# Spreading a gathered token's row into four PSUM banks at once, and sharing three banks between the U and V sums

## The reference

```
q = (t @ wq)                            # 8 heads, 2 halves of 128
s = q . keys ; top 16 of each half ; top 16 of the sums     -> eid, fv
g = softmax(fv)                          # 8 heads x 16 experts per token
hid = gelu(sum_d t[d] * u_tab[eid, d])   # d = 2048
out = sum_e (g * hid)[e] * v_tab[eid, :]
```

## Time and profile before

| what | value |
|---|---|
| median of three executions | 2251.37 us |
| the profiled execution's own time | 2247.8 us |
| its span, first to last instruction | 2246.0 us |
| TensorE busy in the span | 2175.7 us (97%) |
| VectorE busy | 1668.7 us (74%) |
| ScalarE busy | 916.3 us (41%) |
| GpSimd busy | 399.9 us (18%) |
| mean granted clock of TensorE | 0.994 of full speed |

### The profile page before, as it was taken

The page is one execution under the profiler, slowest core; times in us unless marked ns, Lnnn a source line. Parts: engine busy times, 40 slices in busy tenths (PEclk is TensorE's granted clock), DMA queues, the critical chain, the costliest instruction groups (busy, mean ns, idle before and its releaser), DMA issues.

```text
span 2246.0 us, 37321 instructions
## 1 busy us (share of the span) xinstructions
PE 2175.7 (97%) x14886; PEld 1927.0 (86%) x14886; DVE 1668.7 (74%) x3054; ACT 916.3 (41%) x1093; POOL 399.9 (18%) x337
## 2 busy tenths in 40 slices
PE   7899999899999999999999999999999999999996
PEld 1599888678799899999998888999888888989996
DVE  3269777654557899888878878787887877876686
ACT  1332323453443148444434434444343443444444
POOL 1044001300000046011122222222122221211000
PEclk9899999999999999999999999999999999999998
DMA  9957665798844465788899899999999999988763
GB/s 400 416 218 298 261 270 213 297 353 309 356 155 151 153 216 224 275 287 301 310 347 364 339 380 345 352 358 342 358 366 346 361 356 357 338 313 300 284 207 117
DMA packets 113334, 673.49 MB, mean 300 GB/s; under 512 B 12337, under 2 KB 13745, under 8 KB 50321
## 3 DMA queue, kind: packets, MB, share of 16 engines
q1 hardware_dynamic: 77184, 444.63, 52.6%
q0 software_dynamic: 33648, 219.49, 25.8%
q10 hardware_dynamic: 2336, 7.05, 0.8%
HBM read 649.17 MB, written 21.95 MB: 299 GB/s over the span
## 4 chain that ended last, share of the span: by engine, by line
PE 84%; DVE 7%; DMA 6%; ACT 1%; issue 1%; SPq 0%; POOL 0%; DVEq 0%; ACTq 0%
PE vb L1724 17%; PE zb L1709 15%; PE vb L1726 7%; PE zb L1711 7%; PE zb L550 6%; PE zb L552 5%; PE zb L551 5%; PE vb L1758 3%; PE vb L1748 3%; DMA ada_first<-in_w_ada 3%; PE vb L1308 2%; PE vb L1689 2%; PE zb L1665 1%; DVE lo L490 1%; PE vb L1555 1%; PE vb L1723 1%
## 5 line engine op out<-in xcount | busy, mean ns | idle before, releaser
L485 ACT ACTIVATE hi<-raw_two 128x1024 fp32r<-128x1024 f32 x624 | 657.1, 1058 | 966.3 <-PE vb L1724 308.4
L490 DVE TENSOR_TENSOR lo<-raw_two,hi 128x1024 fp32r<-128x1024 f32 x624 | 764.3, 1230 | 276.8 <-ACT hi L485 272.4
L1709 PE MATMUL zb<-act_hl,hi 128*128 128x416 f32 x1792 | 556.4, 368 | 0.0
L1724 PE MATMUL vb<-w_rest,hi 128*128 128x416 f32 x1536 | 495.3, 367 | 0.0
L1711 PE MATMUL zb<-act_hl,lo 128*128 128x208 f32 x1680 | 435.5, 259 | 0.0
L1709 PEld LDWEIGHTS zb<-act_hl,hi 128*128 128x128 f32 x1792 | 334.9, 188 | 35.9 <-issue 24.3
L1726 PE MATMUL vb<-w_rest,lo 128*128 128x208 f32 x1280 | 329.8, 258 | 0.0
L1711 PEld LDWEIGHTS zb<-act_hl,lo 128*128 128x128 f32 x1680 | 320.4, 191 | 5.2
L1724 PEld LDWEIGHTS vb<-w_rest,hi 128*128 128x128 f32 x1536 | 288.5, 188 | 1.4
L550 PE MATMUL zb<-act_hl,hi 128*128 128x288 f32 x960 | 287.8, 300 | 0.4 <-DVEq L1999 0.4
L551 PE MATMUL zb<-act_hl,hi 128*128 128x288 f32 x960 | 282.5, 294 | 0.0
(11 more groups left out here) (301 smaller groups left out, 2721.5 us busy)
## 6 DMA issues: line engine op xcount, KB each, us to landing
raw_two<-in_v SPq DMA_DIRECT2D x128, 1024.0 KB, 7.1
raw_two<-in_u SPq DMA_DIRECT2D x112, 1024.0 KB, 6.4
raw_two<-in_w_in SPq DMA_DIRECT2D x40, 1024.0 KB, 9.6
ada_first<-in_w_ada SPq DMA_DIRECT2D x64, 512.0 KB, 8.7
ada_mid<-in_w_ada SPq DMA_DIRECT2D x64, 512.0 KB, 5.3
ada_late<-in_w_ada SPq DMA_DIRECT2D x64, 512.0 KB, 7.3
raw_two<-in_w_out SPq DMA_DIRECT2D x16, 1024.0 KB, 6.1
raw_two<-in_w_q SPq DMA_DIRECT2D x16, 1024.0 KB, 4.9
```

The source lines that it names most:

```text
L485: act.activation(hi[s][:, :], raw[4 * (q % 2) + s], ACT.Copy).then_inc(hi_ready, 1)
L490: dve.tensor_tensor(lo[4 * (q % 2) + s][:, :], raw[4 * (q % 2) + s], hi[s][:, :].bitcast(F32), ALU.subtract) \
L1709: last = pe.matmul(zb[:, bank, 0:2 * ND], w_h, act_hl[:, k, :, 0:ND], start=(k == 0), stop=(k == KC - 1))
L1724: last = pe.matmul(vb[:, bank, 0:2 * ND], v_h, w[:, e % 2, :, :], start=(e == 0), stop=(e == GI - 1))
```

## The change

The four pieces of a token are spread at once into the four banks of `zb`, and VectorE takes them in one dot of 2048. The U and V sums move out of `zb` and share banks 3, 0 and 1 of `vb` in turn (`SUM_BANKS`), each waiting for the bank's user three places before (`wait_bank`). `add_halves` treats one bank at a time, so there are two for a U quad. All 80 tokens' rows now have the form that the last 16 had: five `twice` tiles, five calls of `turn_tokens`, and `pick_tail` in place of `pick`. The parts of `hid_4` and their reduction are gone. The first two U quads stay in `zb`; the last group's V sums go to `zb`, and the final norm's sum to `vb`.

```diff
-def chunk_unit(c):
-    return 53 * c // 48 - 8
+def spread_unit(t):
+    return 53 * (4 * t + 3) // 48 - 8
...
+SUM_BANKS = (3, 0, 1)
+def z_slot(p, e):
+    if p < PP:
+        return 2 * (p - 2) + e
+    return 4 + 24 * (p // PP - 1) + (e if p % PP == 0 else 16 + 2 * (p % PP) + e)
+def v_slot(g, c):
+    return 4 + 24 * (g - 2) + 2 + c
+def z_bank(p, e):
+    return zb[:, 2 * p + e, :] if p < 2 else vb[:, SUM_BANKS[z_slot(p, e) % 3], :]
+def v_bank(g, c):
+    return vb[:, c % 2, :] if g < 2 else vb[:, SUM_BANKS[v_slot(g, c) % 3], :]
...
 # GpSimd, after the spill of x
-            pool.wait_ge(hs_turned, 1)
-            pool.tensor_copy(twice[:, :, :, :], hF[:, :, ND + NR:T].unsqueeze(2).to_broadcast([P, KC, 2, NT])) \
-                .then_inc(twice_ready, 1)
+            for i in range(5):
+                if i == 4:
+                    pool.wait_ge(hs_turned, 1)
+                tokens = hF[:, :, ND + NT * i:ND + NT * i + NT]
+                pool.tensor_copy(twice[i][:, :, :, :], tokens.unsqueeze(2).to_broadcast([P, KC, 2, NT])) \
+                    .then_inc(twice_ready, 1)
...
 # GpSimd, in the dense loop
-                    for c in chunks_at(n):
-                        t = c // 4
-                        if c % 4 == 3 and t + 2 < NGT:
-                            pool.wait_ge(dots_done, c + 1)
+                    for t in spreads_at(n):
+                        if t + 2 < NGT:
+                            pool.wait_ge(dots_done, t + 1)
                             gather(ug[t % 2], u_rows, t + 2, ug_in[t % 2])
...
 # ScalarE
-                    for r in (0, NR):
-                        last = act.activation(pick[r:r + NR, :], ident[r:r + NR, r:r + NR], ACT.Copy)
-                    last.then_inc(hs_copied, 1)
...
 # TensorE
-            for k in range(KC):
-                for r in (0, NR):
-                    last = pe.matmul(vb[r:r + NR, k // 4, P * (k % 4):P * (k % 4) + P], hF[:, k, ND:ND + NR], ident,
-                                     start=True, stop=True)
+            def turn_tokens(i, bank):
+                pe.wait_ge(twice_ready, i + 1)
+                for kk in range(4):
+                    for j in range(4):
+                        both = twice[i][:, 4 * j + kk, :, :].rearrange("p s t -> p (s t)")
+                        last = pe.matmul(vb[2 * NT * j:2 * NT * j + 2 * NT, bank, P * kk:P * kk + P], both, ident,
+                                         start=True, stop=True)
+                return last
+            for i in range(4):
+                last = turn_tokens(i, i)
             last.then_inc(hs_turned, 1)
-            def turn_tail():
-                pe.wait_ge(twice_ready, 1)
-                for k in range(KC):
-                    j, kk = k // 4, k % 4
-                    last = pe.matmul(vb[2 * NT * j:2 * NT * j + 2 * NT, 2, P * kk:P * kk + P],
-                                     twice[:, k, :, :].rearrange("p s t -> p (s t)"), ident, start=True, stop=True)
-                last.then_inc(hs_turned, 1)
...
-            turn_tail()
+            turn_tokens(4, 2).then_inc(hs_turned, 1)
...
+            def wait_bank(m):
+                if m in (1, 2):
+                    pe.wait_ge(vb_free, 2 + 2 * KC - 2 + m)
+                elif m >= 3:
+                    i, r = divmod(m - 3 - 4, 24)
+                    if m - 3 < 4:
+                        pe.wait_ge(z_sum, 4 + m - 3 + 1)
+                    elif 2 <= r < 2 + KC:
+                        pe.wait_ge(vb_free, 2 + KC * (i + 2) + r - 2 + 1)
+                    else:
+                        pe.wait_ge(z_sum, 8 + 8 * i + (r if r < 2 else r - KC) + 1)
...
-            def spread_row(c):
-                if c == 0:
-                    pe.wait_ge(hs_copied, 3)
+            def spread_token(t):
+                if t == 0:
+                    pe.wait_ge(hs_split, 3)
+                    pe.wait_ge(z_sum, 4)
                 else:
-                    pe.wait_ge(dots_done, c)
...
-                pe.matmul(vb[:, 3, :], one.to_broadcast([P, P]), rows, start=True, stop=True).then_inc(spread, 1)
+                    pe.wait_ge(dots_done, t)
+                i, tt = t // NT, t % NT
+                rows = h_rows[i // 2][:, i % 2, :] if i < 4 else h_tail[:, :]
+                for j in range(4):
+                    last = pe.matmul(zb[:, j, :], pick_tail[:, j, tt:tt + 1].to_broadcast([P, P]), rows, start=True, stop=True)
+                last.then_inc(spread, 1)
...
 # VectorE
-                        rest = h_rows[b2][NR:ROWS, :, :]
-                        dve.tensor_tensor(rest, vb[NR:ROWS, 2 * b2:2 * b2 + 2, :], rest.bitcast(F32), ALU.subtract) \
+                        rows = h_rows[b2][:, :, :]
+                        dve.scalar_tensor_tensor(rows, vb[:, 2 * b2:2 * b2 + 2, :], lo_rows[:, 0:1], rows.bitcast(F32),
+                                                 ALU.mult, ALU.subtract).then_inc(hs_split, 1)
...
-                dve.wait_ge(unit_used, 4 * q + 8)
-                halves = zb[:, 2 * b:2 * b + 2, 0:2 * ND].rearrange("p e (h t) -> p e t h", h=2)
-                dve.tensor_reduce(zs[b][:, :, :], halves, AX_X, ALU.add).then_inc(z_sum, 1)
+                dve.wait_ge(unit_used, 4 * q + 2 * e + 6)
+                halves = z_bank(p, e)[:, 0:2 * ND].rearrange("p (h t) -> p t h", h=2)
+                dve.tensor_reduce(zs[p % 2][:, e, :], halves, AX_X, ALU.add).then_inc(z_sum, 1)
...
-            def dot(c):
-                t, j = c // 4, c % 4
+            def dot(t):
                 b = t % 2
-                dve.wait_ge(spread, c + 1)
-                u = ug[b][:, 512 * j:512 * j + 512]
-                dve.tensor_tensor_reduce(u, u, vb[:, 3, :], 1.0, 0.0, ALU.mult, ALU.add, hid_4[:, c % 64:c % 64 + 1]) \
-                    .then_inc(dots_done, 1)
+                dve.wait_ge(ug_in[b], 8 * (t - b) + 16)
+                dve.wait_ge(spread, t + 1)
+                dve.tensor_tensor_reduce(ug[b][:, :], ug[b][:, :], zb[:, :, :].rearrange("p j x -> p (j x)"), 1.0, 0.0,
+                                         ALU.mult, ALU.add, hid_s[:, t:t + 1]).then_inc(dots_done, 1)
...
-                    if s == 3:
-                        add_halves(q, PP * (g - 2) + pp, pp)
+                    if s >= 2:
+                        add_halves(q, PP * (g - 2) + pp, s - 2)
```

More of the change, by code:

```diff
@@ L112, with spreads_at @@
 LAST_QUADS = 32 * (NG - 3) - 12
-def chunks_at(n):
-    return [c for c in range(4 * NGT) if chunk_unit(c) == n]
+def spreads_at(n):
+    return [t for t in range(NGT) if spread_unit(t) == n]
 def tokens_at(n):
@@ L272, in layer_kernel @@
     vg = [at(f"vg{b}", [P, D], F32, peer + 76160 + 8192 * b) for b in range(2)]
-    h_rows = [at(f"h_rows{b}", [ROWS, 2, 512], F32R, (x_at + 14336, peer + 67968)[b]) for b in range(2)]
+    h_rows = [at(f"h_rows{b}", [P, 2, 512], F32R, (x_at + 14336, peer + 67968)[b]) for b in range(2)]
     h_tail = at("h_tail", [P, 512], F32R, peer + 72064)
-    twice = at("twice", [P, KC, 2, NT], F32, peer + 74112)
-    pick = at("pick", [ROWS, NR], F32R, peer + 96768)
+    twice = [at(f"twice{i}", [P, KC, 2, NT], F32, zone + 45568 + 2048 * i if i < 4 else peer + 74112) for i in range(5)]
     pick_tail = at("pick_tail", [P, 4, NT], F32R, peer + 97024)
@@ L1707, in u_quad @@
                         if k == KC - 1:
-                            pe.matmul(zb[:, bank, 0:ND], w_l, act_hl[:, k, 0, 0:ND], start=False, stop=False)
-                        last = pe.matmul(zb[:, bank, 0:2 * ND], w_h, act_hl[:, k, :, 0:ND], start=(k == 0), stop=(k == KC - 1))
+                            pe.matmul(out[:, 0:ND], w_l, act_hl[:, k, 0, 0:ND], start=False, stop=False)
+                        last = pe.matmul(out[:, 0:2 * ND], w_h, act_hl[:, k, :, 0:ND], start=(k == 0), stop=(k == KC - 1))
                         if k < KC - 1:
-                            last = pe.matmul(zb[:, bank, 0:ND], w_l, act_hl[:, k, 0, 0:ND], start=False, stop=False)
+                            last = pe.matmul(out[:, 0:ND], w_l, act_hl[:, k, 0, 0:ND], start=False, stop=False)
                     last.then_inc(unit_used, 1)
@@ L1714, in u_quad, with v_blocks @@
                         beside(n + s)
-            def v_blocks(q, c, par, bank, e0, e1):
+            def v_blocks(q, c, par, out, e0, e1):
                 s = c % 4
@@ L1722, in v_blocks @@
                     if e == GI - 1:
-                        pe.matmul(vb[:, bank, 0:ND], v_l, w[:, e % 2, 0, :], start=False, stop=False)
-                    last = pe.matmul(vb[:, bank, 0:2 * ND], v_h, w[:, e % 2, :, :], start=(e == 0), stop=(e == GI - 1))
+                        pe.matmul(out[:, 0:ND], v_l, w[:, e % 2, 0, :], start=False, stop=False)
+                    last = pe.matmul(out[:, 0:2 * ND], v_h, w[:, e % 2, :, :], start=(e == 0), stop=(e == GI - 1))
                     if e < GI - 1:
-                        last = pe.matmul(vb[:, bank, 0:ND], v_l, w[:, e % 2, 0, :], start=False, stop=False)
```

(11 more changed lines are left out.)

64 lines of the change are left out of this document (26 added, 38 removed).

## The result

| | before | after |
|---|---|---|
| median on the same chip | 2251.34 us (2250.96 to 2253.24, 5 runs) | 2238.82 us (2238.05 to 2239.47, 5 runs) |
| the profiled execution, span | 2246.0 us | 2237.6 us |

The ratio is 0.9943, with a 95% interval of 0.9929 to 0.9958: the change is faster by 12.5 us. The prediction was 2241.6 us, within 2233 to 2251, and faster.

What follows compares the result with a forecast made beforehand. The prediction took TensorE's stream to bound the kernel. Waits for dots (-4.4), a V sum's wait (-1.6), spreads (-2.4) and turns (-1.4) summed to -9.8 us, from 2251.4 to 2241.6 us, range 2233 to 2251.

Steps and rivals of the forecast that it cites:

- The bound: Dense loop: TensorE's stream sets the pace, so VectorE savings count only where TensorE waits for VectorE.
- Waits for dots, -4.4: Dense loop: eight matmul waits for a dot, restarts included, go; 4.4 us less, bounds 0 and 10.8.
- my upper bound: Waits for dots: 10.8 us saved if the weight loads' 7.6 us of waits counted too.
- Wait for a V sum, -1.6: Dense loop: TensorE's one wait for a V sum's bank goes with three banks; 1.6 us less, bounds 0 and 1.6.
- Spreads in a row, -2.4: Dense loop: 240 spreads following their own kind cost 0.225 us, not 0.235; 2.4 us less, bounds 0 and 5.3.
- Turns, -1.4: Turning token rows on TensorE: 160 rows at 0.030 us, 4.8 in place of 6.2; 1.4 us less.
- the dear price: Rival for the turns: column groups don't overlap, +6.1 us for -1.4, 2249.1 us in all; chance 0.12.
- VectorE, 30 us less: VectorE in the loop: dots 38 us less, `add_halves` 8 us more; worth nothing while TensorE sets the pace.
- Three banks too few: Rival: a four-bank dot at twice the time (4.5 us) delays V units, 36 us more, 2278; chance 0.11 with similar lateness.
- The sum: Whole kernel: -4.4 - 1.6 - 2.4 - 1.4 = -9.8 us, median from 2251.4 to 2241.6 us.

Runs made afterwards that it cites:

- the loops exchanged: Kernel after, with the two loops of `turn_tokens` swapped so four instructions in succession write one column group: 2245.75 us, ratio 0.9979.
- the trace with four dots: Kernel after, with VectorE taking a token's dot as four of 512 and adding the four results: 2238.31 us, ratio 0.9943.
- the pairs: V rows of two value tokens taken in one unit, not one token each: 2227.80 us in the kernel after, 2256.85 us in the kernel before.

## Why the prediction was right

**The bound.** Right. TensorE's stream sets the pace: VectorE's 16 us did nothing, and what shortened TensorE's distances counted in full.

**Waits for dots, -4.4.** The mechanism was right; the term was probably somewhat small. By starts, 5.3 us went ahead of the spreads of the kernel before, 4.5 of them at the eight waits counted. One bank in place of four costs 3.2 us by medians and 6.3 by the profiled loops, on both sides of 4.4. Part of the loss lies behind a spread and not ahead of it, where I didn't look: a lone spread takes 0.2333 us to the next start with four banks, 0.2374 with one, and 0.2402 in the kernel before, and 320 x 0.007 = 2.2 us. I had put that down to the shape of a lone spread. That the weight loads' waits, my upper bound, are its cause was not tested. Which loads land late differs between executions, so the term has no fixed size.

**Wait for a V sum, -1.6.** Right: gone, and with two banks back at 1.5 us.

**Spreads in a row, -2.4.** Too large: at most 1.7 us, 1.0 without the other wait. A lone spread without a wait costs 0.2333, near the 0.235 taken, but a spread in a row costs 0.232, not 0.225; the 0.012 us on top of streaming of the earlier trace rows became 0.019. The Trainium skill (TensorE: Matmul & The Clock Gate, Back-to-back issue gap) gives 216 ns for 512 columns as the gap of an isolated matmul, and about 131 in a sustained stream of weight loads and matmuls. Four spreads show 927 ns, 232 each, so neither fits here, and the measurement decides. The two terms together were 6.8, and the grouping of starts gives 8.0: the sum came out near because one term was too small and the other too large, which is luck.

**Turns, -1.4.** Right: 3.71 + 2.46 became 3.70 + 1.08. The rival, the dear price by the order of the groups, was tested with the loops exchanged and is real: 5.7 us for the other order. The Trainium skill (TensorEngine Tiling (Array Packing), Key Properties) has tiles that load and multiply independently; the 0.029 and 0.063 us a row agree with that, and the order decided here which of the two it was.

**VectorE, 30 us less.** Only 14.8 less, with no effect on the time. I priced the old dot at 0.69, but in a row of four such dots starts are 0.61 apart (1418.15, 1418.76, 1419.37 in the trace with four dots), and a long dot takes 2.21 to the next start: 80 x (2.44 - 2.21) = 18 us, not 38. Less the 8 us for `add_halves` that leaves 10, so some 5 of the 14.8 aren't explained. On VectorE as on TensorE the distance between starts was the price here, not the duration.

**Three banks too few.** The rival's edge fits (no loss at 3.5 us, a loss at 4.6), its dot was not: four banks are read at the usual rate. The Trainium skill's advice (Perfetto Trace Analysis, Matmul Optimizations) to use all eight PSUM banks spoke for the rival. Here three are enough for the sums and two are not, by 5.2 us.

**The sum.** -8.4 was predicted for the dense loop, -10.1 came; -1.4 for the turns came as predicted; the tail gave 0.3. The medians differ by 12.5, 0.7 more than the stages; that much differs between executions. Of the 2.8 us by which the kernel is faster than 2241.6, 1.7 are the loop.

## What to carry to other kernels

A bank that is refilled only after its reader is done ties the producer to everything that stands ahead of that reader in its queue. Buying slack there (here four banks against one) paid twice here: the waits went, and edits that make the reader later at times, like the pairs, turned from a loss of 5.2 us in the loop into a gain of 12.6. And count a repeated operation by the distance between starts in the place where it stands, not by its duration.

## What the runs showed of the hardware

- A burst of 128x32 matmuls between 128x128 ones costs 0.08 us to enter and 0.08 to leave, and two bursts of 8 joined into one of 16 take 0.15 us less beyond that: 12.6 us for 40 pairs.
- Matmuls of 32 columns of the array, each with its weight load: 0.029 us a row when the column group changes with each instruction, 0.063 when it changes with every fourth; only the order of the same 128 instructions differs.
- A VectorE step that reads 2048 elements across four PSUM banks takes 2.287 us, 1.05 ns for each element beyond the 512 of one bank (0.681 us).
